# Second attention layer of a two-layer decoder: values made with tokens as rows, output units split by row tiles, routing rows on ScalarE

## The reference, cut to what matters

```
# layer 1, attention: 16 heads of 64, keys and values from a shared latent c (256 wide)
q, c_kv, q_idx, k_idx, w_idx, qc = split_cols(h @ odd_w_in, ...)
c = rmsnorm(c_kv, odd_kv_norm)
# an indexer scores all causal keys; the best 64 per query are kept
logits = q @ (c W_uk)^T / 8 + bias;  p = softmax(logits over the kept keys)
o = p @ (c W_uv)                     # values = c W_uv per head
# 4 more heads attend to a memory of 256 rows
x = x + concat(o, cross) @ w_out     # 1280 -> 1024
# layer 1, experts
t = rmsnorm(x); logits = t @ w_router; the two best experts of 8, weights by softmax
y = sum over e of gate_e * ((silu(t @ w_gate[e]) * (t @ w_up[e])) @ w_down[e])   # 1024 -> 3584 -> 1024
```

## Time and profile before

| | us |
|---|---|
| median of three timed runs | 1551.38 |
| profiled execution, time | 1550.68 |
| profiled execution, span from first to last instruction | 1548.9 |
| TensorE busy in the span | 1519.9 |
| VectorE busy | 1319.2 |
| ScalarE busy | 1125.1 |
| GpSimd busy | 101.5 |

### The profile page before, as it was taken

One profiled execution on the slowest core, in us unless ns is written; L12 is line 12 of the kernel. 1 busy time (PEld: TensorE's weight loads), 2 busy tenths in 40 slices (PEclk: granted clock), 3 DMA queues, 4 the chain that ended last, 5 costly groups with the idle time before them and its releaser, 6 DMA issues.

```text
span 1548.9 us, 25105 instructions
## 1 busy us (share of the span) xinstructions
PE 1519.9 (98%) x8156; PEld 1285.6 (83%) x8156; DVE 1319.2 (85%) x1784; ACT 1125.1 (73%) x1500; POOL 101.5 (7%) x73
## 2 busy tenths in 40 slices
PE   9999999999999999999999999999999999999997
PEld 8999967888888778888888888888888888888885
DVE  5888868777768869998998998998998998998996
ACT  6565556444456758888788788788888878878875
POOL 2422100000021011000000000000000000000000
PEclk9999999999999999999999999999999999999999
DMA  9944436666633378999999999999999999999992
GB/s 286 233 136 136 151 98 202 182 192 184 175 88 84 130 300 309 406 378 383 380 374 382 377 397 364 379 399 356 388 393 357 388 395 353 392 393 351 399 386 106
DMA packets 227062, 455.40 MB, mean 294 GB/s; under 512 B 12912, under 2 KB 120576, under 8 KB 227008
## 3 DMA queue, kind: packets, MB, share of 16 engines
q1 hardware_dynamic: 222800, 439.52, 78.5%
q0 software_dynamic: 4208, 15.22, 3.9%
HBM read 445.52 MB, written 9.18 MB: 294 GB/s over the span
## 4 chain that ended last, share of the span: by engine, by line
PE 94%; DVE 2%; ACT 2%; issue 1%; DMA 0%; SPq 0%; ACTq 0%; DVEq 0%
PE ps L804 27%; PE ps L806 26%; PE ps L805 26%; PE ps L1110 5%; PE ps L1112 2%; PE ps L912 2%; PE ps L1295 2%; PE ps L943 1%; PE ps L928 1%; DVE w_lo L1783 0%; ACT w_hi L1332 0%; PE ps L1237 0%; PE ps L1228 0%; PE ps L840 0%; ACT pr L1422 0%
## 5 line engine op out<-in xcount | busy, mean ns | idle before, releaser
L1783 DVE TENSOR_TENSOR w_lo<-big,w_hi 128x1024 fp32r<-128x1024 f32 (+2 forms) x833 | 980.4, 1216 | 130.0 <-ACT w_hi L1679 53.1
L1679 ACT CAST w_hi<-big 128x1024 fp32r<-128x1024 f32 x672 | 693.5, 1056 | 141.1 <-PE ps L806 138.0
L804 PE MATMUL ps<-w_hi,m_hi 128*128 128x512 f32 (+1 forms) x1008 | 391.7, 389 | 1.5 <-issue 1.4
L806 PE MATMUL ps<-w_hi,m_lo 128*128 128x512 f32 (+1 forms) x1008 | 389.4, 386 | 0.0
L805 PE MATMUL ps<-w_lo,m_hi 128*128 128x512 f32 (+1 forms) x1008 | 389.2, 386 | 0.0
L804 PEld LDWEIGHTS ps<-w_hi,m_hi 128*128 128x128 f32 x1008 | 189.6, 188 | 41.3 <-issue 3.7
L806 PEld LDWEIGHTS ps<-w_hi,m_lo 128*128 128x128 f32 x1008 | 189.6, 188 | 38.2
L805 PEld LDWEIGHTS ps<-w_lo,m_hi 128*128 128x128 f32 x1008 | 189.7, 188 | 37.2
L1332 ACT CAST w_hi<-big 128x1024 fp32r<-128x1024 f32 (+2 forms) x170 | 165.9, 985 | 37.4 <-PE ps L806 33.8
L804 PE MATMUL ps<-w_hi,h_two 128*128 128x512 f32 (+1 forms) x464 | 181.9, 392 | 0.0
L806 PE MATMUL ps<-w_hi,h_two 128*128 128x512 f32 (+1 forms) x464 | 179.3, 386 | 0.0
(11 more groups left out here) (298 smaller groups left out, 1581.4 us busy)
## 6 DMA issues: line engine op xcount, KB each, us to landing
big<-in_odd_w_gate SPq DMA_DIRECT2D x112, 1024.0 KB, 7.4
big<-in_odd_w_up SPq DMA_DIRECT2D x112, 1024.0 KB, 7.4
big<-in_odd_w_down SPq DMA_DIRECT2D x112, 1024.0 KB, 7.5
big<-in_even_w_in SPq DMA_DIRECT2D x42, 512.0 KB, 4.2
big<-in_even_w_gate SPq DMA_DIRECT2D x22, 512.0 KB, 4.5
big<-in_even_w_up SPq DMA_DIRECT2D x22, 512.0 KB, 3.9
big<-in_even_w_down SPq DMA_DIRECT2D x22, 512.0 KB, 4.6
big<-in_w_out SPq DMA_DIRECT2D x20, 512.0 KB, 3.6
```

The costliest lines, as they stand in the source:

```text
L804: mm(dst, a[0], b[0], start=start, stop=False, **kw)
L806: return mm(dst, a[1], b[0], start=False, stop=stop, **kw)
L1679: nc.scalar.copy(w_hi[:, slot, :], ring[s][:, (u % 2) * UNIT:(u % 2 + 1) * UNIT]).then_inc(s_hi, 1)
L1783: return V.tensor_tensor(dst, src, lead.bitcast(F32), ALU.subtract)
```

## The change

- `PROJ` and `step_projections`: values are made for two pairs at once, `("v", m)` for pairs 2m and 2m+1, in odd steps; the first one ahead of pair 0. The latent is now the operand that is loaded into TensorE and the weights stream, so the result has tokens as rows. ScalarE copies 512 columns once into one of two places in `big` (`values_of`, columns 6144 to 7168, in the ring's part). `turn_values` and `values_odd` are gone from layer 1.
- SyncE's first ring loads wait for the mix of pair 7, since the values lie in the ring's first place.
- `step_odd`: up to pair 6 both heads are turned ahead of the next scores, with a bank each; from pair 7 on, an output unit is cut in two by row tiles, tile 0 ahead of head 1's turn and tile 1 behind it. In step 9 unit 6 follows ahead of the mix. Units 8 and 9 come last.
- Ahead of pair 0, ScalarE runs one tiny exp before it copies the first keys out, the first exps of pair 0 come before the copy of query 3, and the low part of the latent is made in round 6 and not 7 (counted from 0).
- Six filler products, not four. The first gather goes to four banks (1, 3, 4, 5), two chunks each, with semaphores of its own (`s_gat0`, `s_ghi0`). VectorE's `tables` come behind the gathered tokens. `y_out(0)` waits for them too.
- ScalarE scales the routing rows, behind the exp of the gates; GpSimd only saves them.

In the diff, a line "..." marks what is left out.

```diff
@@ -147,16 +147,17 @@
 MADE_IN = {g: g + AHEAD + 1 for g in range(NPAIR - AHEAD - 1)}
-PROJ = [("q", 0), ("q", 1), ("q", 2), ("k", 0), ("v", 0), ("k", 1), ("q", 3), ("v", 1), ("q", 4)]
+PROJ = [("q", 0), ("q", 1), ("q", 2), ("k", 0), ("k", 1), ("v", 0), ("q", 3), ("q", 4)]
...
-        ([("v", g + 2)] if g + 2 < PAIRS else [])
+        ([("v", g // 2 + 1)] if g % 2 and g + 2 < PAIRS else [])
@@ -165,8 +166,9 @@
 OUT_MADE = {5: (0,), 6: (1, 2), 7: (3, 4), 8: (5, 6, 7), 9: (8, 9)}
-OUT_USED = {6: ((), (0,)), 7: ((), (1, 2)), 8: ((), (3, 4)), 9: ((5,), (6, 7, 8))}
+OUT_USED = {6: (None, 0), 7: (1, 2), 8: (3, 4), 9: (5, 7)}
@@ -504,7 +507,7 @@
         def one_bank(pair):
-            return pair.kind == "even" or pair.gs[-1] >= (LATE, OUT_FROM)[pair.l]
+            return pair.kind == "even" or pair.gs[-1] >= (LATE, OUT_FROM + 1)[pair.l]
@@ -535,6 +538,9 @@
             return (1, 3)[c // 4]
+        def first_bank(c):
+            return ps[:, (1, 3, 4, 5)[c // 2], (c % 2) * P:(c % 2 + 1) * P]
@@ -549,8 +555,12 @@
             return (zq[:, 512:768], zq[:, 768:1024], kiT, qT[:, 0, 0, :])[g - 2 * NBR]
+        def values_of(m):
+            return big[:, 6144 + 512 * (m % 2):6144 + 512 * (m % 2 + 1)].rearrange("p (t n) -> p t n", t=TT)
...
-            return U.at[("proj", *key)], RC * P if key[0] != "q" else UNIT
+            return U.at[("proj", *key)], {"q": UNIT, "k": RC * P, "v": 2 * RC * P}[key[0]]
@@ -658,7 +668,8 @@
                 else:
-                    load(0, 0, [u], (w_uk if what == "k" else w_uv)[:, :, g * P:(g + 1) * P], n)
+                    m = n // RC
+                    load(0, 0, [u], (w_uk if what == "k" else w_uv)[:, :, g * m:(g + 1) * m], n)
@@ -679,7 +690,7 @@
             load(0, 0, [U.at[("router", 0)]], w_router, NARROW)
-            sp.wait_ge(s_at[1]["scores_read"], 2 * PAIRS + 1)
+            sp.wait_ge(s_at[1]["mixed"], 2 * PAIRS + 1)
@@ -764,10 +775,6 @@
             save(sum_rows, X, 0)
-            pool.wait_ge(s_used, U.at[("router", 0)] + 1)
-            pool.wait_ge(s_rstd, NORM_FFN1 + 1)
-            for t in range(TT):
-                nc.gpsimd.tensor_scalar(XH[:, t, :], X[:, t, :], rstd[:, t:t + 1], None, ALU.mult).then_inc(s_xrow, 1)
@@ -870,11 +877,19 @@
                 u, width_ = proj_unit(key)
-                product(ps[:, 3 + n % 2, 0:SEQ], split(0, 0, [u], kc, width_), src, kc)
+                w = split(0, 0, [u], kc, width_)
+                if key[0] != "v":
+                    product(ps[:, 3 + n % 2, 0:SEQ], w, src, kc)
+                    return
+                for t in range(TT):
+                    for c in range(RC):
+                        last = mm3(ps[:, 3 + n % 2, t * SEQ:(t + 1) * SEQ], part(CS, A_, c, tok(t)), part(w, A_, c, A_),
+                                   t == 0 and c == 0, c == RC - 1, skip_group_check=True)
+                last.then_inc(s_used, 1)
...
-                pe.wait_ge(S["evacuated"], pair.before() + pair.mats if pair.l == 0 else PROJ_AT["v", pair.g] + 1)
+                pe.wait_ge(S["evacuated"], pair.before() + pair.mats)
@@ -933,9 +948,14 @@
                 pe.wait_ge(S["mix_lo"], pair.g + 1)
-                if not pair.cross:
+                if pair.cross:
+                    v = vx[:, pair.l * XPAIRS + pair.gs[0] - PAIRS, :, :]
+                elif pair.l == 0:
...
-                v = (vx[:, pair.l * XPAIRS + pair.gs[0] - PAIRS, :, :] if pair.cross else vN[:, :, :])
+                    v = vN[:, :, :]
+                else:
+                    pe.wait_ge(S["evacuated"], PROJ_AT["v", pair.g // 2] + 1)
+                    v = values_of(pair.g // 2)[:, :, (pair.g % 2) * P:(pair.g % 2 + 1) * P]
@@ -945,25 +965,24 @@
                             last.then_inc(S["mixed"], 1)
-            def out_unit(l, ch):
+            def out_unit(l, ch, tiles=range(TT)):
...
-                    else:
-                        pe.wait_ge(s_at[l]["values"], PAIRS)
...
-                for t in range(TT):
+                for t in tiles:
...
-                last.then_inc(s_used, 1)
+                if tiles[-1] == TT - 1:
+                    last.then_inc(s_used, 1)
@@ -1015,26 +1034,26 @@
                 now = pair_at(1, g)
-                first, second = OUT_USED.get(g, ((), ()))
+                amid, behind = OUT_USED.get(g, (None, None))
...
-                for ch in first:
-                    out_unit(1, ch)
-                if g < OUT_FROM:
+                if g <= OUT_FROM:
...
-                if g >= OUT_FROM:
+                if g > OUT_FROM:
+                    out_unit(1, amid, (0,))
...
+                    out_unit(1, amid, (1,))
+                    if g + 1 == NPAIR:
+                        out_unit(1, amid + 1)
...
-                if g + 1 < PAIRS:
-                    turn_values(pair_at(1, g + 1))
...
-                for ch in second:
-                    out_unit(1, ch)
+                if behind is not None:
+                    out_unit(1, behind)
@@ -1047,10 +1066,10 @@
                         scores(pair_at(1, 0))
-                        turn_values(pair_at(1, 0))
...
-                out_unit(1, NPAIR - 1)
+                for ch in range(NPAIR - XPAIRS, NPAIR):
+                    out_unit(1, ch)
@@ -1211,7 +1230,7 @@
             last.then_inc(s_used, 1)
-            for _ in range(4):
+            for _ in range(6):
@@ -1225,10 +1244,10 @@
                     for t in range(TT):
-                        last = mm(ps[:, gather_bank(c), (c % 4) * P:(c % 4 + 1) * P], X[:, t, c * P:(c + 1) * P],
+                        last = mm(first_bank(c), X[:, t, c * P:(c + 1) * P],
...
-                    if c % 4 == 3:
-                        last.then_inc(s_gat, 1)
+                    if c % 2:
+                        last.then_inc(s_gat0, 1)
@@ -1403,10 +1422,10 @@
                 else:
-                    if g >= 1:
-                        act.wait_ge(S["turned_v"], g)
-                    dst = vT[:, :]
-                nc.scalar.copy(dst, ps[:, 3 + n % 2, 0:SEQ]).then_inc(S["evacuated"], 1)
+                    if g >= 2:
+                        act.wait_ge(S["mixed"], 4 * g - 3)
+                    dst = values_of(g).rearrange("p t n -> p (t n)")
+                nc.scalar.copy(dst, ps[:, 3 + n % 2, 0:(2 if what == "v" else 1) * SEQ]).then_inc(S["evacuated"], 1)
@@ -1480,10 +1499,6 @@
                 nc.scalar.copy(m_hi[:, g, :], ps[:, 6, 0:SEQ]).then_inc(S["mix_hi"], 1)
-            def values_odd(g):
-                act.wait_ge(s_at[1]["turned_v"], g + 1)
-                nc.scalar.copy(vN[:, :, :].rearrange("p t n -> p (t n)"), value_bank(pair_at(1, g))).then_inc(s_at[1]["values"], 1)
@@ -1494,8 +1509,6 @@
                     mix_hi(g)
-                    if g + 1 < PAIRS:
-                        values_odd(g + 1)
@@ -1633,12 +1646,12 @@
             hi_odd(("k", 0))
-            hi_odd(("v", 0))
+            hi_odd(("k", 1))
...
-            hi_odd(("k", 1))
+            hi_odd(("v", 0))
@@ -1652,20 +1665,17 @@
             act.sem_inc(s_at[1]["probsT"], 1)
-            hi_odd(("v", 1))
...
+            A(small[:, 56:57], con[:, C_ONES:C_ONES + 1], ACT.Exp)
...
+            evac_odd(("k", 1))
+            for key in step_projections(0):
+                hi_odd(key)
...
-            evac_odd(("k", 1))
-            values_odd(0)
-            for key in step_projections(0)[:2]:
-                hi_odd(key)
+            exps(pair_at(1, 0), 0)
...
-            exps(pair_at(1, 0), 0)
-            evac_odd(("v", 1))
...
-            hi_odd(step_projections(0)[2])
@@ -1704,12 +1714,15 @@
             A(ex2, dlt, ACT.Exp).then_inc(s_ex2, 1)
+            act.wait_ge(s_used, U.at[("router", 0)] + 1)
+            for t in range(TT):
+                A(XH[:, t, :], X[:, t, :], ACT.Copy, scale=rstd[:, t:t + 1]).then_inc(s_xrow, 1)
...
-                        act.wait_ge(s_gat, 2 * p + c // 4 + 1)
+                        act.wait_ge(s_gat, 2 * p + c // 4 - 1)
@@ -1750,11 +1763,17 @@
                         expert_hi(u, p + 1)
-            gathered(0)
+            for c in range(DC):
+                if c % 2 == 0:
+                    act.wait_ge(s_gat0, c // 2 + 1)
+                last = A(g_hi[:, c, :], first_bank(c), ACT.Copy, scale=gn[:, G_FFN1 + c:G_FFN1 + c + 1])
+                if c % 2:
+                    last.then_inc(s_ghi0, 1)
...
+            act.wait_ge(s_glo, 2)
@@ -2087,7 +2106,7 @@
                     V.reciprocal(rstd, sd).then_inc(s_wie, 1)
-                if k == 7:
+                if k == 6:
@@ -2259,10 +2278,8 @@
                 for c in range(DC):
-                    if c == DC // 2 and isinstance(p, int) and p == 0:
-                        tables()
...
-                        dve.wait_ge(s_ghi, 2 * p + c // 4 + 1)
+                        dve.wait_ge(s_ghi, 2 * p + c // 4 - 1)
@@ -2302,7 +2319,13 @@
                         expert_lo(u, p + 1)
-            gathered(0)
+            for c in range(DC):
+                if c % 2 == 0:
```

(6 more changed lines are left out.)

## The result

The changed kernel takes 1544.23 us (median of 5 runs, 1539.77 to 1545.43); the kernel before took 1551.65 beside it (5 runs, 1551.24 to 1553.58). The ratio is 0.9944, 95% interval 0.9931 to 0.9956. Forecast was 1547.2: the direction was right and the time lies just inside the range, whose lower end is 1544.0. But the gain is much larger than the 4.2 us of the sum: 7.4 us between the medians, and 8.7 us by the ratio.

What follows compares the result with a forecast made beforehand. TensorE, busy for 98% of the span, was taken as the bound, so an earlier first expert product ends the kernel earlier. Attention's -4.76 us and the fillers' +0.6 gave -4.2 us, with 1547.2 us predicted, range 1544.0 to 1550.4.

Steps and rivals of the forecast that it cites:

- Part 1: Attention ahead of pair 0: reordered work leaves its scores at 473.5 and nets -0.25 us, bounds -1.1 and +0.5.
- Part 2: Attention steps 0 to 4: no turns of values, steps of 6.62 and 8.04 us; -1.66 us, bounds -2.9 and -0.3.
- rival D: VectorE and ScalarE become the bound in odd attention steps and output steps; 1549.1 us, chance 0.12.
- Part 3: Attention steps 5 and 6: the first output unit no longer waits for copied values; -2.35 us, bounds -2.9 and -1.2.
- Part 4: Steps 7 to 9: half output units cover copy waits of 1.92 us, new waits of 0.9 and 0.5; 0.5 us gained.
- Part 5: Routing stage: +0.6 us for two more fillers, zero for the four-bank gather and for rows moved to ScalarE.
- three long instructions: Routing: tiny VectorE instructions beside GpSimd's work should shrink, 2.5 us in all; not taken into the sum.
- The fillers: Routing: two more filler products cost up to 0.86 us at 1.2 GHz, nothing at 2.4 GHz; taken as +0.6.
- Rival B: Routing: the fillers bring the clock back before or early in the gather; -7.4 us, 1544.0 us, chance 0.12.
- Rival C: Routing: the clock falls amid the router's narrow products, costing 1 to 2.5 us more; 1549.0 us, chance 0.16.
- Rival E: Routing: clock low from before the router's products into the expert products; +1.1 us, 1552.5, or +3.6 with D's gains; chance 0.08.

Runs made afterwards that it cites:

- Experiment 12: The kernel before, unchanged, run once more for a second profiled execution: 1551.91 us, ratio 1.0002.
- 9: The kernel before with only the scaling of the routing rows moved from GpSimd to ScalarE: 1549.35 us against 1551.60, ratio 0.9989.
- experiment 6: The changed kernel with the scaling of the routing rows put back on GpSimd: 1546.61 us, ratio 0.9967 to the kernel before.
- experiment 5: The changed kernel, unaltered, run once more: 1544.00 us, ratio 0.9950 to the kernel before.
- Experiment 11: The changed kernel with GpSimd also doing two scalings into tiles that nobody reads: 1545.91 us, ratio 0.9959 to the kernel before.
- 2: The kernel before with the routing part alone (six fillers, four-bank gather, tables behind it, rows on ScalarE): 1549.45 us against 1551.25, ratio 0.9991.
- 4: The changed kernel with eight more filler products among the router's narrow products: 1544.90 us, ratio 0.9959 to the kernel before.

## Why the prediction fell short

Its own steps, in order.

**Part 1** (-0.25, scores at 473.5, both sets of turns from 481.8): 473.58 and 481.73, with no wait. Right.

**Part 2** (-1.66; steps of 6.62 and 8.04): 6.62 and 8.06, and pair 5 begins 1.95 us earlier, 517.71 for 519.66, where parts 1 and 2 said 1.91. Right; rival D is out.

**Part 3** (-2.35): the wait of 0.9 us for head 1 of pair 6 measured 0.60, and the output unit starts at 526.55, 4.15 us earlier, where 4.26 was forecast. Right in each execution that stays at the full clock. Missed: the same gap let the clock fall in some executions of the kernel before, 2.8 us each time, if the gap is the cause. With two in five, a count too small to trust, that is 1.1 us on the mean.

**Part 4** (-0.5; new waits of 0.9 and 0.5): 4.63 - 4.15 = 0.48, waits 0.70 and 0.38. Right in sum. At the router 4.63 for 4.76.

**Part 5** is the step that failed: the rows moved off GpSimd were put at zero. That "while the gather runs at 1.2 GHz a faster VectorE gives nothing" was said of one profiled execution and put into the sum as if every execution had 10 us of low clock there. In others it has 7, 3 or none; there VectorE sets the end of the stage, and GpSimd sets VectorE. Experiment 12 shows that at 10 us, too, the first expert product can wait for VectorE. The zero measured 2.2 us (9 against its runs of before) and 2.6 (6 against 5) in medians, 16.86 - 15.61 = 1.25 in the means of profiled stages, and 1.1 and 0.4 there at equal low clock. So 1.3 to 2.6 with what clock goes with it, against "2.5 us in all" for the three long instructions; that figure was in the prediction, and not taken. (A fourth, a TENSOR_TENSOR of 0.91 us from 578.79, was overlooked; it ends with the 0.98 of the earlier trace rows and costs nothing more.)

How much of it is VectorE's wait and how much the clock isn't settled. Between 6 and 5 the mean clock differs by 0.0023, which at 1.15 us for 0.001 (last section) would make the 2.6 us by itself; only 9 has its gain at nearly the same clock. Why the clock should stay up more often without GpSimd's rows, or whether that was chance, the runs don't show.

The Trainium skill (SBUF — State Buffer, "Who interferes with whom"), cited in the prediction for an exclusive lock between GpSimd and some VectorE forms, was the rule that spoke for it. Experiment 11 agrees, with 0.99 and 1.06 us beside GpSimd and 0.17 without. I can't say from these runs which forms are free of it.

**The fillers** (+0.6): six, four or none gave 1544.0, 1543.9 and 1543.2, and six for four in the kernel before nothing. So zero, within the 2 us or so that the intervals leave open. In single stages at an equal 10 us of low clock six cost 0.4 us over four (16.77 and 16.36), less than the 0.6. The Trainium skill (TensorE: Matmul & The Clock Gate, part 1) puts the release of the clock down to sustained activity and not to a count of matmuls; that two fillers more were worth nothing in either kernel agrees.

**The rivals.** Rival B named nearly the right time, 1544.0, and its price is the lower end of the range: that 1544.23 lies inside it is luck. Its mechanism is neither shown nor out. The whole gather ran at 2.4 GHz (3.84 us) in three executions, of kernels with six or with fourteen fillers (2, 5 and 4), in none of the six with four or none, but not in five others with six either; and the time is the same with six, four or none. Rival C's mechanism is in the first profile (narrow products 4.51 us) and cost 0.86 us there, which the gather got back. Rival E's "+3.6" counts the fillers twice: its own terms give 5.9 - 2.9 = 3.0.

**The end of the kernel** was not looked at. The last store lands sooner. Its row in the view of DMA issues, in experiment 12 and then in 5 (last column: us to landing):

```profile
out<-XH SPq DMA_DIRECT2D x2, 512.0 KB, 3.4
```

```profile
out<-XH SPq DMA_DIRECT2D x2, 512.0 KB, 2.9
```

With some 0.2 us around it the span ends 0.7 us closer to the last normalization, in all kernels with the attention part but for experiment 6 (3.2 us to landing there).

**The sum again**, by what was measured: attention 4.7, with its clock 1.1 more; rows 1.3 to 2.6; end 0.7; fillers 0. That makes 7.8 to 9.1 with the clock term and 6.7 to 8.0 without. Measured: 7.4 by medians; 0.0056 of 1551.65, so 8.7 (6.8 to 10.7), by the first ratio; 7.8 (5.9 to 9.8) by that of experiment 5. The 3.2 us that the forecast lacked are the rows' (taken as zero), the end's 0.7, the fillers' 0.6 and, less surely, the clock in attention. The medians behind these terms hold some clock of their own, so the terms overlap.

None of the variants beats the changed kernel by more than the runs can tell; that without fillers equals it and is shorter.

## What to carry to other kernels

Where a profiled stage sits on a low granted clock, cost an edit there for the full clock too, since the next execution may have it: ask which engine would be last if TensorE ran at 2.4 GHz. Take GpSimd work away from beside a chain of tiny VectorE instructions even if that chain seems hidden. And before trusting a difference of profiles below 0.5%, take a second profile of each kernel and compare by stages: here the attention stages that kept the full clock agree to 0.1 us within one order of work, while whole spans of one program differ by 3.

## What the runs showed of the hardware

One program's granted clock is not the same from execution to execution. The changed kernel's first five runs had mean clocks of 0.994 to 0.999 and took 1545.43 to 1539.77 us; within the kernels of this case, all 14 taken together, a mean clock 0.001 higher goes with 1.15 us less. Where it falls is also open: in the first profile of the changed kernel it fell while TensorE was busy with 8-column products, in experiment 5 it stayed at 1.00 through the same products.

The time from the start to pair 0's scores, in code that hardly differs up to there, ran from 470.50 to 475.92 us. Experiment 12 was 2.4 us late there, with no more low clock than the first profile: one early product waited 2.25 us for its low half, which waited 0.51 us in the first.

Why the last store is quicker was not tried. The traces show one thing that goes with it in all 14 executions. The view of DMA queues has one instruction fetch near the store. In the six executions whose end takes 7.0 or 7.1 us (experiment 6 among them) it comes 2.0 to 2.5 us after the store is issued, amid its data; in the eight at 6.4 or 6.5 us it comes within the first 1.0 us. So the layout of the code may be the cause, by way of when that fetch falls. That is argued, not shown.
